# Rows of the experts' first two matrices laid eight to a partition

## What is computed

```python
D_MODEL = 1024; MOE_GROUPS = 4; MOE_EXPERTS_PER_GROUP = 8; MOE_TOP_K = 2; MOE_HIDDEN = 512

def hier_moe(x, w_group, b_group, w_expert, b_expert, w1, w3, w2):
    ...
    gates = jnp.sum(jax.nn.one_hot(expert_id, N_EXPERTS, dtype=f32) * weight[..., None], axis=1)

    def step(acc, ew):
        w1e, w3e, w2e, ge = ew
        h = jax.nn.silu(xt @ w1e) * (xt @ w3e)
        return acc + ge[:, None] * (h @ w2e).astype(f32), None

    y, _ = lax.scan(step, jnp.zeros((t, d), f32), (w1, w3, w2, gates.T))
    return y.astype(x.dtype).reshape(b, s, d)
```

## Time and profile before

| | us |
|---|---|
| median of 3 runs | 2823.86 |
| lowest and highest | 2822.52, 2825.3 |
| span of the profiled execution, first to last instruction | 2819.0 |

### The profile page before, as it was taken

One profiled execution on the slowest core, in us unless ns is written; L12 is line 12 of the kernel. 1 busy time (PEld: TensorE's weight loads), 2 busy tenths in 40 slices (PEclk: granted clock), 3 DMA queues, 4 the chain that ended last, 5 costly groups with the idle time before them and its releaser, 6 DMA issues.

```text
span 2819.0 us, 30761 instructions
## 1 busy us (share of the span) xinstructions
PE 2512.3 (89%) x12481; PEld 1598.0 (57%) x12482; DVE 800.3 (28%) x1338; ACT 628.9 (22%) x1012; POOL 164.9 (6%) x90
## 2 busy tenths in 40 slices
PE   7878999999979979999897897898999968878998
PEld 6544444444356644443333785556887847744996
DVE  1252011010020221011002546524232326354444
ACT  1121010101000610111102312423222224224334
POOL 0000000000000000000000325000000004240000
PEclk9988999999989989999999988899999988789999
DMA  8675976999966669999999001300323140130351
GB/s 326 260 276 187 393 286 231 393 393 394 396 250 243 233 242 385 394 393 393 395 396 359 1 1 60 123 1 22 113 90 120 45 163 1 60 117 7 135 199 71
DMA packets 241920, 602.27 MB, mean 214 GB/s; under 512 B 12679, under 2 KB 21751, under 8 KB 241824
## 3 DMA queue, kind: packets, MB, share of 16 engines
q1 hardware_dynamic: 241824, 600.91, 56.7%
HBM read 598.25 MB, written 2.64 MB: 213 GB/s over the span
## 4 chain that ended last, share of the span: by engine, by line
PE 70%; SPq 14%; DVE 6%; DMA 4%; ACT 2%; issue 2%; POOL 1%; DVEq 0%; ACTq 0%; POOLq 0%
PE ps L1756 13%; SPq L647 13%; PE ps L752 10%; PE ps L1565 8%; PE ps L1772 7%; PE ps L759 6%; PE ps L214 4%; PE ps L735 3%; PE ps L727 3%; PE ps L223 3%; PE ps L1738 3%; DMA ring<-in_moe_w_dram 1%; PE ps L1689 1%; PE ps L1709 1%; PE ps L313 1%
## 5 line engine op out<-in xcount | busy, mean ns | idle before, releaser
L752 PE MATMUL ps<-ring,arena 128*64 128x512 f32 x2176 | 477.2, 595 | 20.6 <-DMA ring<-in_moe_w_dram 18.7
L1756 PE MATMUL ps<-ring_r,ring_r 128*128 128x512 f32 (+1 forms) x2112 | 372.1, 339 | 12.5 <-DVE ring_r L2090 12.5
L1756 PEld LDWEIGHTS ps<-ring_r,ring_r 128*128 128x128 f32 x2112 | 329.0, 192 | 54.8 <-DVE ring_r L2090 13.1
L752 PEld LDWEIGHTS ps<-ring,arena 128*64 128x64 f32 x2176 | 155.9, 137 | 335.1 <-issue 305.8
L759 PE MATMUL ps<-ring,arena 128*64 128x512 f32 x1088 | 248.5, 598 | 26.8 <-ACT arena L817 13.8
L1565 PE MATMUL ps<-ring_r,ring_r 128*128 128x512 f32 (+2 forms) x1056 | 217.7, 367 | 8.9 <-DVE ring_r L1975 8.9
L1289 POOL TENSOR_TENSOR ring_r<-ring,ring_r 128x1024 fp32r<-128x1024 f32 (+2 forms) x28 | 85.9, 3088 | 2180.6 <-ACT ring_r L1284 2180.6
L1565 PEld LDWEIGHTS ps<-ring_r,ring_r 128*128 128x128 f32 x1056 | 189.1, 212 | 37.4 <-issue 9.3
L1772 PE MATMUL ps<-ring_r,ring_r 128*128 128x512 f32 x480 | 157.4, 401 | 12.3 <-DVE arena_r L1332 12.3
L759 PEld LDWEIGHTS ps<-ring,arena 128*64 128x64 f32 x1088 | 76.4, 137 | 151.2 <-issue 130.3
L907 DVE TENSOR_TENSOR arena<-ps,arena 128x512 f32<-128x512 f32 x34 | 23.6, 693 | 470.0 <-PE ps L752 470.0
(11 more groups left out here) (321 smaller groups left out, 2500.1 us busy)
## 6 DMA issues: line engine op xcount, KB each, us to landing
ring<-in_moe_w_dram SPq DMA_DIRECT2D x192, 2048.0 KB, 19.3
ring<-in_w_mod_dram SPq DMA_DIRECT2D x24, 2048.0 KB, 13.5
ring<-in_w_gate_dram SPq DMA_DIRECT2D x10, 2048.0 KB, 9.1
ring<-in_w_up_dram SPq DMA_DIRECT2D x10, 2048.0 KB, 14.2
ring<-in_w_in_dram SPq DMA_DIRECT2D x8, 2048.0 KB, 14.8
ring<-in_w_down_dram SPq DMA_DIRECT2D x8, 2048.0 KB, 11.4
ring<-in_w_out_dram SPq DMA_DIRECT2D x4, 2048.0 KB, 10.1
ring<-in_w_down_dram SPq DMA_DIRECT2D x4, 1536.0 KB, 8.1
```

What stands on the lines that cost most here:

```text
L752: ins = pe.matmul(PS[CAP * e:CAP * e + CAP, 2 + c, :], xeT[:, k, CAP * e:CAP * e + CAP], w[c][:, e, k, :], start=(k == 0), stop=(k == KT - 1))
L1756: ins = pe.matmul(PS[:, 2 * (i % GU_BANKS) + a, 0:ntok], w[:, k, a, :], as_r(x[:, k, 0:ntok]), start=(k == 0 and n == 0), stop=(k == KT - ...
```

## The change

The first and second matrices are laid out with eight neighbouring rows on a partition: row 8p + k lies on partition p at step k. A partition's part of such a matrix is then one run of 4096 numbers, 16 KB, in the DRAM and in `ring`. The third matrix is laid out as before. The gather has to give the same rows at step k, and takes columns k, k + 8, k + 16, ... of X instead of 128 neighbouring ones.

```diff
-        w_up = lambda name, e: t[name][layer, e, :, :].rearrange("a (k p) n -> p (a k) n", p=P)
+        def w_up(name, e):
+
+            w = t[name][layer, e, :, :]
+            return w.rearrange("a (k p) n -> p (a k) n", p=P) if name == "moe_w2" else w.rearrange("a (p k) n -> p (a k) n", p=P)
...
                 for k in range(KT):
                     for tt in range(NT):
-                        ins = pe.matmul(PS[:, 2 + k // 4, (k % 4) * P:(k % 4 + 1) * P], X[:, tt, k * P:(k + 1) * P],
+                        ins = pe.matmul(PS[:, 2 + k // 4, (k % 4) * P:(k % 4 + 1) * P], X[:, tt, k:D:KT],
                                         view(sel[:, tt, 0, 0:1], [1, P]), start=(tt == 0), stop=(tt == NT - 1))
```

## The result

The changed kernel takes 2946.97 us (median of 4 runs, 2938.4 to 2950.51), the kernel before 2824.58 us (4 runs, 2822.52 to 2826.35) beside it. The ratio is 1.0435, with a 95% interval of 1.042 to 1.045: 122 us slower. The forecast was 2797 us and the range ended at 2850 us, so both are wrong, and the sign too.

What follows compares the result with a forecast made beforehand. TensorE was taken to pace early expert rounds (29.82 us), transfers (31.91 us a pair) the later ones. Gains of 5.7 + 17.5 + 3.7 = 26.9 us off the 2823.9 us median gave 2797 us; range 2789 to 2850 us.

Steps and rivals of the forecast that it cites:

- The gather, costed at nothing: Gather's stepped weight loads in the expert loops: no extra cost taken, bounds 0 and 110 ns a load.
- Rival 1: Stepped read doubles the gather load's column time: 3.5 us a gather, +127 us, 2924 us; chance 0.15 in full.
- the pace term: Router products L709 of layer 1, with the wait gone, run at layer 0's pace: 1.7 us more gained.
- The transfers: Expert loads of first and second matrices: 16 KB pieces cut a transfer from 5.42 to 4.90 us.
- Rivals 2 to 4: Long pieces slower (2882 us, 0.04); pieces cost less than thought (2803 us, 0.08); queue still cuts to 2 KB (2824 us, 0.05).
- Rival 3: A piece costs less than two rates say: transfer 5.22 us, gain 20.6 us, 2803 us; chance 0.08.
- layer 0's lead: Head start the four-slot ring gives layer 0's transfers before TensorE waits: put at 23.7 us.
- What the loops get back: Expert loops paced by TensorE alone to the last round: 5.7 us gained in layer 0, 17.5 us in layer 1.
- Ahead of layer 1's loop: Router products start earlier as small router loads land sooner, then run at layer 0's pace: 3.7 us together, bounds 0 and 3.7.
- The sum of 3.7 us: Whole gain forecast ahead of layer 1's loop: the router's wait gone (2.0 us) plus layer 0's pace (1.7 us).
- The level: Whole program: median run time taken to stay 4.9 us above the profiled span of 2819.0 us.

Runs made afterwards that it cites:

- the loads alone: Kernel before with only the loads changed to 16 KB pieces, gather left contiguous (wrong rows paired, time only): 2804.09 us, ratio 0.9927.
- The kernel with the sorted norm: Changed kernel's 16 KB pieces, but layer norms write and read X in the pieces' order, so the gather reads neighbouring columns: 2806.77 us, ratio 0.9947.

## Why the prediction was wrong, step by step

*The gather, costed at nothing: this step failed.* Its reason was that 0.86 ns are two cycles of a column at 2.4 GHz, so that a read of one word has time to spare. The observation was right, the conclusion was not: the pace per column says how fast columns go in when four of them share a line, and nothing on what a line costs. The trace of before had no TensorE read with a step. The rule of the Trainium skill that the prediction quotes spoke against the change, and the full price was given a chance of 0.15 where the loads stood back to back and 23 ns a load were enough to decide. The measured price is 126 ns a load.

*Rival 1 was the outcome,* and a little too small: 3.5 us a gather was taken from the column time alone (110 ns a load), and 4.04 us came. 36 x 0.54 = 19 us of the 23 us by which its 2924 us missed; the rest is the pace term below and what varies in the last stages.

*The transfers: right.* 4.90 us from a line through two rates; 426 to 434 GB/s measured, 4.83 to 4.92 us. 8 KB pieces gave 424 GB/s where the same line gives 4.82 + 0.15 = 4.97 us, 422 GB/s. The Trainium skill's cost per packet (DMA: Bandwidth & Descriptors, Why small descriptors are slow), about 3 cycles or 3.5 ns by estimate, doesn't fit: it would have left a transfer at 5.22 us, and from 2 KB to 16 KB the traces show 0.50 to 0.59 us for 56 pieces fewer on each engine, 9 to 10.5 ns a piece. Rivals 2 to 4 fell with it. (Rival 3 took layer 0's lead from the 14 rounds of layer 1, though layer 0 has 18 rounds for its 16 pairs; 23.7 us is therefore not shown, and the forecast doesn't rest on it.)

*What the loops get back: right.* 5.7 and 17.5 us forecast, 5.7 and 17.4 us in the loads alone. In after they are there too, under 17 and 15 slower gathers.

*Ahead of layer 1's loop: half right.* The wait for the small router load went, as forecast. The timeline of after:

```profile
1077.45 0.82 PE L712 MATMUL ps<-arena 128*128 128x36 f32 x3 [0.88 <-DVE arena L202]
```

The idle time is 0.88 us behind DVE instead of 2.90 us behind the DMA: 2.0 us. The further 1.7 us, from L709 lasting as long as in layer 0, didn't come: L712 took 7.03 us. The windows over L709 of before, layer 0 and layer 1, then over L712 of after in layer 1:

```profile
224.00:229.00 5.00, 4.83 (x32) 4.68 (x32) 0.56 (x3) 0.00 (x0) 0.00 (x0) 0.74 0.79 302
1006.80:1012.80 6.00, 5.93 (x32) 5.78 (x32) 0.00 (x0) 0.00 (x0) 0.00 (x0) 0.60 0.98 367
```

```profile
1077.40:1084.50 7.10, 7.01 (x32) 6.90 (x32) 0.57 (x3) 0.00 (x0) 0.00 (x0) 0.50 1.04 416
```

The length goes with the granted clock: 4.83 us at 0.74, 5.93 at 0.60, 7.01 at 0.50, the lower of the two levels, 1.2 GHz, throughout. The prediction took a duration that the clock had made for one that the wait had made. The kernel with the sorted norm had the same 32 rows of layer 1 in 4.61 us at a clock of 0.79. The loads alone show 7.02 us as well, and still 3.6 us less between the loops: the 1.1 us that L712 takes longer come back in the eight rows of L724 behind it (6.03 us before, 4.97 us there), 2.0 are the wait, and 1.7 are the 256 products of L214 in layer 1's attention, 57.17 us long before and 57.18 us in after. The windows over them, of before and then of the loads alone:

```profile
815.00:872.00 57.00, 56.17 (x266) 49.04 (x268) 4.13 (x6) 3.53 (x6) 0.00 (x0) 0.98 0.25 92
```

```profile
810.00:866.00 56.00, 55.49 (x256) 48.55 (x256) 3.91 (x7) 3.54 (x6) 0.00 (x0) 1.00 0.20 75
```

At a clock of 1.00 they take 55.49 us. The sum of 3.7 us was met there by another cause than the one named.

*The level.* The profiled execution of after took 2948.95 us with a span of 2947.2 us, 1.8 us lie around it. If that holds for the one of before, it took some 2820.8 us, 3 us under the median, an estimate; the 4.9 us of the prediction was then 1.8 us of surroundings and 3.1 us of what varies. The sum doesn't change by it.

## What to carry to other kernels

Before a layout is chosen for the DMA's sake, ask which operand is then read with a step, and how many of its elements share 16 bytes: with two fp32 numbers a line TensorE's loads took 5% longer, with one 107 to 111%. Longer pieces need only be long enough for the transfers to fall under the bound engine's round; here 4 KB gave nearly all that 16 KB did, and the rest of the trade was pure cost. Where an operation stands back to back on the engine that sets the pace, an unmeasured price per element on it is to be carried as a main case, not as a rival with a small chance.

## What the runs showed of the hardware

TensorE takes 1.84 to 1.88 ns for each new 16-byte line of an fp32 operand, stationary (177 ns for 128 columns with 96 lines, 240 ns with 128) or moving (241 ns, one run), and never under 0.89 ns a column. DVE pays 0.66 to 0.69 ns an element for steps of 512 bytes, on top of some 1.3 ns. Pieces of 2, 4, 8 and 16 KB moved 387, 410, 424 to 427 and 426 to 434 GB/s in windows that held one kind alone. Whether a 2-byte operand pays by the line in the same way wasn't tried, nor a version that writes X in an order that needs no stepping at all with 4 KB pieces.
